# Two modulation units fewer in the first feed-forward's first iteration, the second query block scaled inside the norm, one PE wait left out

## The reference, cut to what matters

```
cond = jax.nn.silu(c)
mod = (cond @ ada_w[l] + ada_b[l]).reshape(B, N_SUBLAYERS, 3, D_MODEL)
h = modulate(x, norm_g[l, 0], mod[:, 0, 0], mod[:, 0, 1])
x = x + 0.5 * mod[:, 0, 2][:, None, :] * swiglu(h, ffn1_w1[l], ffn1_w3[l], ffn1_w2[l])
h = modulate(x, norm_g[l, 1], mod[:, 1, 0], mod[:, 1, 1])
z = h @ w_in          # fox queries fq are its first 512 columns
fq = rms_norm(fq.reshape(B, S, FOX_HEADS, HEAD_DIM), fox_qk_g[0])
```

## Time and profile before

| | |
|---|---|
| Times | 2002.37, 2000.66, 1999.92 us; median 2000.66 |
| Profiled execution | 2001.95 us, its span 1999.9 us |
| Granted TensorE clock, mean | 0.993 |
| PE busy | 1949.8 us (97% of the span) |
| DVE, ACT, POOL busy | 973.2, 765.7, 859.7 us |
| Chain that ended last | PE 78%, issue 10%, POOL 5%, DVE 4% |

### The profile page before, as it was taken

The page is one execution under the profiler, slowest core; times in us unless marked ns, Lnnn a source line. Parts: engine busy times, 40 slices in busy tenths (PEclk is TensorE's granted clock), DMA queues, the critical chain, the costliest instruction groups (busy, mean ns, idle before and its releaser), DMA issues.

```text
span 1999.9 us, 25498 instructions
## 1 busy us (share of the span) xinstructions
PE 1949.8 (97%) x9182; PEld 1543.0 (77%) x9182; DVE 973.2 (49%) x1532; ACT 765.7 (38%) x1270; POOL 859.7 (43%) x382
## 2 busy tenths in 40 slices
PE   7999999999999999989999999899999999999998
PEld 6877666688888888868888887676667888888887
DVE  6763565432642465677672234767882364101111
ACT  5343455433431232433313325445664343222321
POOL 3365221243544344635544445334343454443442
PEclk9999999999999999999999999999999999999999
DMA  6355111243656477648643353323122533343341
GB/s 172 95 137 135 34 43 43 53 100 104 173 152 192 122 184 209 165 119 213 163 114 86 92 148 73 74 57 79 25 63 54 146 86 95 96 104 95 85 114 53
DMA packets 160903, 217.45 MB, mean 109 GB/s; under 512 B 15624, under 2 KB 135976, under 8 KB 160680
## 3 DMA queue, kind: packets, MB, share of 16 engines
q1 hardware_dynamic: 140232, 167.34, 33.5%
q10 hardware_dynamic: 20576, 48.83, 8.2%
HBM read 212.98 MB, written 2.10 MB: 108 GB/s over the span
## 4 chain that ended last, share of the span: by engine, by line
PE 78%; issue 10%; POOL 5%; DVE 4%; ACT 2%; DMA 1%; ACTq 0%; POOLq 0%; SPq 0%; DVEq 0%
PE ps L701 23%; PE ps L703 23%; PE ps L702 23%; POOL wlo L634 4%; PE ps L1100 1%; PE ps L1126 1%; PE ps L1113 1%; PE ps L1199 1%; PE ps L791 1%; PE ps L1223 1%; PE ps L985 0%; PE ps L975 0%; DMA xrow<-in_x 0%; DVE st L2126 0%; DVE score L2572 0%
## 5 line engine op out<-in xcount | busy, mean ns | idle before, releaser
L634 POOL TENSOR_TENSOR wlo<-raw,whi 128x1024 fp32r<-128x1024 f32 (+1 forms) x317 | 782.1, 2484 | 998.1 <-ACT whi L1509 975.6
L701 PE MATMUL ps<-hhi,whi 128*128 128x512 f32 x1400 | 556.5, 398 | 15.2 <-POOL wlo L634 11.8
L703 PE MATMUL ps<-hhi,wlo 128*128 128x512 f32 x1400 | 547.5, 391 | 0.0
L702 PE MATMUL ps<-hlo,whi 128*128 128x512 f32 x1400 | 547.1, 391 | 0.0
L1509 ACT ACTIVATE whi<-raw 128x1024 fp32r<-128x1024 f32 x309 | 317.2, 1056 | 384.5 <-PE ps L703 341.6
L701 PEld LDWEIGHTS ps<-hhi,whi 128*128 128x128 f32 x1400 | 264.4, 189 | 77.4 <-issue 12.5
L703 PEld LDWEIGHTS ps<-hhi,wlo 128*128 128x128 f32 x1400 | 264.0, 189 | 56.0
L702 PEld LDWEIGHTS ps<-hlo,whi 128*128 128x128 f32 x1400 | 264.4, 189 | 54.3 <-issue 1.4
L701 PE MATMUL ps<-hidhi,whi 128*128 (+1 forms) x608 | 236.6, 389 | 0.0
L703 PE MATMUL ps<-hidhi,wlo 128*128 (+1 forms) x608 | 236.5, 389 | 0.0
L702 PE MATMUL ps<-hidlo,whi 128*128 (+1 forms) x608 | 236.5, 389 | 0.0
(11 more groups left out here) (453 smaller groups left out, 2619.2 us busy)
## 6 DMA issues: line engine op xcount, KB each, us to landing
raw<-in_ffn_w SPq DMA_DIRECT2D x264, 256.0 KB, 3.9
raw<-in_w_in SPq DMA_DIRECT2D x154, 256.0 KB, 3.9
trig<-in_ada_w ACTq DMA_DIRECT2D x72, 512.0 KB, 4.8
raw<-in_w_up SPq DMA_DIRECT2D x64, 256.0 KB, 4.0
raw<-in_w_down SPq DMA_DIRECT2D x64, 256.0 KB, 3.8
raw<-in_w_out SPq DMA_DIRECT2D x32, 256.0 KB, 3.8
early_w<-in_ffn_w ACTq DMA_DIRECT2D x8, 512.0 KB, 8.8
xrow<-in_x ACTq DMA_DIRECT2D x4, 512.0 KB, 7.2
```

Source lines behind the costliest of these rows:

```text
L634: last = pool.tensor_tensor(lo, src, hi.bitcast(F32), ALU.subtract)
L701: pe.matmul(out_, lhi, rhi, start=first, stop=False)
L702: pe.matmul(out_, lhi, rlo, start=False, stop=False)
L703: return pe.matmul(out_, llo, rhi, start=False, stop=last)
```

## The change

The tables of units are other ones: iteration 0 adds units 48 and 49 at its end instead of 48 to 51, iterations 3 and 4 add three units instead of two in their middle, and the units between move accordingly. DVE's second pair of query results is computed in the norm after chunk 5 instead of behind it. PE no longer waits on `bias_ready` after block n = 1.

```diff
-        MOD_MID = [(0, 0), (52, 54), (57, 59), (62, 64), (67, 69), (0, 0)]
-        MOD_END = [(48, 52), (54, 57), (59, 62), (64, 67), (69, 72), (0, 0)]
+        MOD_MID = [(0, 0), (50, 52), (55, 57), (60, 63), (66, 69), (0, 0)]
+        MOD_END = [(48, 50), (52, 55), (57, 60), (63, 66), (69, 72), (0, 0)]
...
                             if unscaled and n == 1:
                                 shift_sums(4, 1)
-                                pe.wait_ge(bias_ready, 2 * STAT[4])
...
-            norm(4, {3: lambda: first_queries(0)})
-            first_queries(1)
+            norm(4, {3: lambda: first_queries(0), 5: lambda: first_queries(1)})
```

## The result

The changed kernel takes 1990.25 us (median of 5 runs, 1989.32 to 1991.64) beside 2000.85 for the kernel before, measured side by side: a ratio of 0.9947, 95% interval 0.9936 to 0.9957, or 10.6 us less. 1989.0 was forecast. The profiled execution took 1990.96, its span is 1989.1. From the wait that went (line 847) on, the lines of the source are one lower here: L2126 of before is L2125.

A forecast was written before the change was run, and what follows sets the result against it. PE was taken to bound the kernel, busy 1949.8 of 1999.9 us, so only its stalls could pay. Gains of 6.3 and 5.6 us, together 11.9, from the median 2000.66 gave 1988.8, forecast as 1989.0, range 1985.0 to 1995.0.

The forecast's parts named there:

- the escape to 892.3: Before feed-forward iteration 2: POOL's first low part may avoid colliding with DVE's additions, so PE starts at 892.3, not 893.2.
- The clock behind it: After the wait before iteration 2: the clock probably stays at 1.00, winning back 2.7 us (0 to 2.7).
- (a): Block 6's turn before iteration 3: PE may wait for unit 55; charged 0.6 us, ends 0 and 4.
- (b): Middles of iterations 3 and 4: the third unit mostly fills DVE's idle time; cost nothing, otherwise up to 2 us each.
- (c): Block 8's turn: PE, arriving earlier, may wait for unit 71; charged 1.2 us, ends 0 and 4.
- the 0.5 us: High parts of iterations 4 and 5 on ACT still queue behind three loads each; some 0.5 us charged.
- The first part: Gain from the feed-forward's stall before iteration 2, after charges: 6.3 us, ends 2.5 and 9.0.
- the second part: Gain from removing the bias stall at the queries, limited by DVE's reciprocals: 5.6 us, ends 3.5 and 9.8.
- One: Feed-forward: the units set the pace and the first part is mostly given back; 7 us gained, 1993.5; chance 0.18.
- Two: Queries: the second part is kept whole, as PE needn't wait for the dsa query; 16 us gained, 1984.6; chance 0.10.
- Three: Middles of iterations 3 and 4: DVE and ACT fall behind, pace per unit worsens; slower, 2006; chance 0.04.
- four: Before iteration 2: ACT still holds the slab for another reason, leaving only the second part; 1995.2; chance 0.05.

The follow-up runs named there:

- empty iteration 0: The changed kernel with no unit added at the end of iteration 0, three in iteration 1's middle and four at its end: 1993.78 us, ratio 0.9951.
- the tables alone: The kernel before with only the new unit tables, without the query edits: 1995.57 us against 2001.99, ratio 0.9973.
- early roots: The changed kernel with ACT's roots for queries 0 and 1 taken in the norm after chunk 5: 1987.85 us, ratio 0.9927; later run 1986.98, 0.9930.
- the hook: DVE's second query pair inside the norm after chunk 5; alone on the kernel before, bias wait kept: 1997.20 us, ratio 0.9981.
- half additions: The kernel with early roots, DVE adding only 512 of 1024 columns of units 50 to 71: 1983.41 us, ratio 0.9905.

## Why the prediction came out right, point by point

**The wait before iteration 2** was put at 2.3 to 3.2 us, measured 3.14. ACT's high part was expected at 888.8 and stands at 888.81, PE at 893.2 and stands at 893.20. The low parts kept their collision, so the escape to 892.3 didn't come: 5.5 us, not the 5.9 taken. That two waits are long "of all" was not so: the list of before has a third of 7.5 us, for the input's DMA (L1447). It is 7.6 after, and plays no part.

**The clock behind it** is the first step that failed. "A wait of this size probably leaves it there" was argued from a window inside the stall, in which the clock was 1.00. It was 1.00 there after the change too, and yet 0.72 in 893 to 899. The clock in the first 3 us of a stall doesn't tell what it is once PE has restarted. 2.7 us were booked, 1.1 came.

**(a), (b), (c) and the 0.5 us** made 2.3 us of charges, and the changed kernel's profile has no wait at the turns of blocks 6 and 8. On DVE's side the steps were right: unit 55 was to be done at 915 to 916 and was at 915.61, unit 71 at 979 to 980 and was at 980.10. On PE's side they weren't: PE was to be at block 6's turn at 915.5 and came at 917.54, and at block 8's not at 979 (986.74 - 8.6 = 978.1 by its own sum) but at 980.16. It was late by the 0.4 us of the wait and the 1.6 us of the clock, 2.0 in all, and so found both units done. The first part was thus booked 2.0 us too high before the charges and charged 2.3 us that nobody paid as waits: 6.3 forecast, 6.5 measured. That they cancel is in part luck, and in part not: with unit 71 at 980.10, a PE that was 1.6 us earlier would have stood for it about 1.5 us (an estimate from these rows). So the turn of block 8, forecast at 980.4 and measured at 980.16, is right for reasons that were partly wrong. The places were right, as the wait of 5.0 at block 6 with an empty iteration 0 shows, and those of 2.6 and 2.1 at block 8 in the profiles of the tables alone and of the first run with early roots.

**The queries up to block 3.** PE at 1263.0 to 1264.3 less the first part's gain was forecast as 7.5 to 8.8 us ahead; it is 8.4, with a wait of 2.50 for the forecast 3. The 0.7 us for query 1 weren't lost. That queries 2 and 3 don't move on ACT was argued; the 18.9 us with and without the hook show it. What the prediction didn't say is that the hook is then worth nothing that the runs can tell beside the other edit. The runs of the single edits had to show it.

**What is late next** was named rightly: the chain of reciprocals. The idle times were forecast at 1.7 us each and are 1.79, and the product behind the dsa query came 5.9 us earlier for the forecast 5.7, with a wait of 2.74 for the forecast 2 to 3. The early roots, which start just this chain earlier, shortened the stretch by 5.3 us more.

**The second step that failed** is a term that is missing: the half clock behind that new wait, 1.8 us. Hence 4.1 us and not 5.6 for the second part. Why the clock fell behind the waits of 3.14 and 2.74 and not behind that of 2.50, the runs don't settle. Length alone doesn't decide: waits of 1.96, 2.08, 2.52, 2.62, 2.65, 2.74, 2.77, 2.84 and 3.14 us were followed by slow products somewhere in these runs, and those of 2.33 and of 2.47 to 2.51 (the low part at block 3, in five kernels) were not.

**The rivals.** One (the units' pace) doesn't hold for this change, but begins 0.06 us behind it: in the profile of every try to win more at the first stall the time was lost again to another unit or low part. (Its own terms, 8.6 - 4 - 4 - 0.5, would have left 0.1 us of the first part and not 1 to 2.) Two fell to the new wait for ACT. Three is excluded by the 6.6 us at block 8, and four by ACT's high part at 888.81.

## What to carry to other kernels

When a stall goes, put a price on the next wait in full, with the half clock behind it, and not only its length: of the changed kernel's three long waits those of 3.14 and 2.74 us cost 1.6 and 1.8 us more, and that of 2.50 nothing. Look, too, at how much margin the next place has left: a gain that ends 0.06 us short of the next wait can't be added to. Of two edits that aim at the same stall, ask what each gives if the other is in; the smaller one may be worth nothing. And look at who feeds the engine that is late next: moving two roots of 0.6 us shortened the stretch behind the norm by 5.3 us, where the two query edits together had taken 4.1 off it (in the times, 3.4 to 4.0 us against 4.8).

## What the runs showed of the hardware

The slow stretch begins up to 1.3 us after PE has restarted (first slow product at 894.46 behind a start at 893.20, or already the first one at 966.73) and held seven to nine products where all of them were of L701 to L703. In the changed kernel it cost 1.6 us behind the wait of 3.14 and 1.8 behind that of 2.74. A granted clock of 1.00 in the wait says nothing of the clock behind it: it was 1.00 in the waits of 3.14 and 2.50 us alike, and fell to 0.50 behind the first alone.

An addition on DVE that starts while POOL runs a low part does not run slower, it stands until 0.2 us before the low part's end (21 of 21 in two profiles) and then takes its own 1.28 us, or 0.75 when it is half as long. One that starts first takes its own time, and the low part grows from 2.39 to up to 3.38 us.

The spread of the times was itself a finding: the changed kernel's five runs lie within 2.3 us, those of the tables alone within 11, and those with half additions within 1.7. That the collisions cause a part of it isn't shown: half additions were timed only four times, and their spread is hardly narrower than the changed kernel's. The wait of 2.77 us at 849.72, ahead of every edit, comes from something that wasn't tried.
